# Expert weights laid out and requested in three pieces of 2 MB with runs of 16384 B, in place of six of 1 MB with runs of 8192 B

## What is computed

```python
def _moe(h, router_g, router_e, w1, w3, w2):
    ...
    expert = g_idx * E_PER_GROUP + e_idx          # each token: 2 of 32 experts
    ...
    def block(args):
        tok, e = args
        xb = h[tok]
        return (jax.nn.silu(xb @ w1[e]) * (xb @ w3[e])) @ w2[e]
    ...
    y = jnp.zeros((T, D_MODEL), jnp.float32).at[slot_tok].add(
        out.reshape(-1, D_MODEL).astype(jnp.float32) * slot_w[:, None])
```

## Time and profile before

| | us |
|---|---|
| median of 3 executions | 1469.42 (1469.12 to 1469.8) |
| the profiled execution, its time | 1473.97 |
| its span | 1472.1 |
| expert stage, from the first `up` to the last matmul of a block | 894.69 to 1422.53 |
| PE busy | 1368.9 (93%) |

### The profile page before, as it was taken

How to read it: one execution, slowest core, us unless ns; L and a number is a source line. 1 busy time by engine, 2 the same in 40 slices (tenths; PEclk the granted TensorE clock), 3 DMA queues, 4 the chain that set the end, 5 groups by cost and what they waited for, 6 DMA issues and landing times. The chain is left out here.

```text
span 1472.1 us, 33644 instructions
## 1 busy us (share of the span) xinstructions
PE 1368.9 (93%) x13661; PEld 960.7 (65%) x13661; DVE 671.2 (46%) x1362; ACT 309.4 (21%) x843; POOL 566.1 (38%) x452
## 2 busy tenths in 40 slices
PE   8999999998998999999999858999999989999864
PEld 4678888865566668887777534666666766666641
DVE  4757787842325567666667471112112111111127
ACT  1311011113113444443443100011001001100015
POOL 4212423402223235543334012445545544445435
PEclk9999999999998999999999979999999999999987
DMA  6334333244136232213321199999999999999936
GB/s 250 89 97 99 76 78 102 61 121 160 47 110 245 90 100 80 86 66 115 115 94 44 72 396 376 388 399 399 396 396 404 395 395 398 395 395 395 392 87 237
DMA packets 129606, 318.04 MB, mean 216 GB/s; under 512 B 48120, under 2 KB 86512, under 8 KB 103672
## 3 DMA queue, kind: packets, MB, share of 16 engines
q1 hardware_dynamic: 109720, 294.35, 53.3%
q0 software_dynamic: 18656, 18.15, 5.7%
q10 hardware_dynamic: 1152, 4.52, 0.8%
HBM read 277.05 MB, written 47.74 MB: 221 GB/s over the span
## 5 line engine op out<-in xcount | busy, mean ns | idle before, releaser
L2660 PE MATMUL bank<-sb_arena 128*32 128x256 f32 x6144 | 341.5, 381 | 12.2 <-DVE sb_arena L2768 5.7
L2660 PEld LDWEIGHTS bank<-sb_arena 128*32 128x32 f32 x6144 | 222.9, 111 | 125.4 <-issue 13.2
L515 PE MATMUL bank<-sb_arena 128*128 128x276 f32 x1008 | 235.0, 395 | 0.0
L2631 POOL DMA_INDIRECT d_acc<-sb_arena,sb_oidx x96 | 152.1, 1584 | 194.0 <-ACT sb_arena L2726 166.0
L515 PEld LDWEIGHTS bank<-sb_arena 128*128 128x128 f32 x1008 | 191.0, 190 | 44.0
L2676 PE MATMUL bank<-sb_arena 128*32 128x256 f32 x3072 | 172.9, 379 | 7.7 <-ACT sb_arena L2726 7.6
L2676 PEld LDWEIGHTS bank<-sb_arena 128*32 128x32 f32 x3072 | 110.6, 110 | 66.4 <-ACT sb_arena L2726 9.9
L2624 POOL DMA_INDIRECT sb_arena<-d_x,sb_idx x99 | 102.6, 1037 | 109.4 <-DVE sb_idx L2754 51.8
L2773 DVE TENSOR_SCALAR sb_oidx<-sb_slot 128x3 int32 x32 | 5.6, 174 | 286.1 <-DMA d_acc<-sb_arena,sb_oidx 285.7
L2726 ACT ACTIVATE sb_arena<-bank,sb_arena 128x256 f32<-128x256 f32 x96 | 38.5, 472 | 397.1 <-DVE sb_arena L2774 387.7
L1281 PE MATMUL bank<-sb_arena 128*128 128x512 f32 (+1 forms) x256 | 119.7, 596 | 0.0
(11 more groups left out here) (420 smaller groups left out, 1842.5 us busy)
## 6 DMA issues: line engine op xcount, KB each, us to landing
sb_arena<-w SPq DMA_DIRECT2D x192, 1024.0 KB, 28.1
sb_arena<-w_conv SPq DMA_DIRECT2D x28, 512.0 KB, 4.8
sb_arena<-d_conv SPq DMA_DIRECT2D x7, 1792.0 KB, 7.3
d_conv<-sb_arena SPq DMA_DIRECT2D x22, 512.0 KB, 3.3
sb_arena<-d_gam SPq DMA_DIRECT2D x8, 768.0 KB, 5.2
d_x<-sb_arena SPq DMA_DIRECT2D x9, 512.0 KB, 2.6
sb_arena<-xT ACTq DMA_DIRECT2D x8, 552.0 KB, 9.3
sb_arena<-w_out SPq DMA_DIRECT2D x8, 512.0 KB, 7.9
```

The lines of the kernel that those rows point to most:

```text
L515: last = e.matmul(bank[at + t][:, 0:HT // 2], weights[:, k, :], x[:, k, HT // 2 * t:HT // 2 * t + HT // 2], start=(k == 0), stop=(k == HK ...
L2631: e.indirect_dma_start(rows_out, bass.IndirectOffsetOnAxis(ap=oidx[:, r:r + 1], axis=0), eo[:, r, :], None, bounds_check=LAST_ROW, oob_is_ ...
L2660: mm = e.matmul(bank[UPB + r][j * CG:(j + 1) * CG, 0:2 * P], xgT[:, 2 * q + k, r * CG:(r + 1) * CG], w13[s][q][:, k, j, :], start=(q == 0 ...
```

## The change

The weights are laid out anew in memory, so that a request of 2 MB has one contiguous run of 16384 B for each partition. `w13` of an expert comes in two halves where it had four quarters, `w2` in one piece where it had two halves. SP waits until PE has passed the whole of the larger piece before it requests its refill, and PE waits once for each piece. The bytes, the order of the experts, the matmuls and the three sets stay. All else in the program is as it was.

```diff
-                    for q in range(4):
-                        e.dma_start(w13[s][q].rearrange("p k j n -> p (k j n)"), a["w13"][s, q]).then_inc(W["w13" + "abcd"[q] + str(s)], 16)
                     for h in range(2):
-                        e.dma_start(w2[s][h].rearrange("p k n -> p (k n)"), a["w2"][s, h]).then_inc(W["w2" + "ab"[h] + str(s)], 16)
+                        e.dma_start(w13[s][h].rearrange("p k j n -> p (k j n)"), a["w13"][s, h]).then_inc(W["w13" + "ab"[h] + str(s)], 16)
+                    e.dma_start(w2[s].rearrange("p k n -> p (k n)"), a["w2"][s]).then_inc(W["w2" + str(s)], 16)
...
                 def first_down(n, ex):
-                    for h in range(2):
-                        e.wait_ge(S["e_out"], 2 * (n - NSET) + h + 1)
-                        later2(h, n % NSET, ex)
+                    e.wait_ge(S["e_out"], 2 * (n - NSET) + 2)
+                    later2(n % NSET, ex)
...
                 for n in range(NSET, E1):
                     ex = expert(n)
-                    for q in range(4):
-                        e.wait_ge(S["e_up"], 4 * (n - NSET) + q + 1)
-                        later13(q, n % NSET, ex)
+                    for h in range(2):
+                        e.wait_ge(S["e_up"], 4 * (n - NSET) + 2 * h + 2)
+                        later13(h, n % NSET, ex)
...
                     for q in range(4):
-                        e.wait_ge(W["w13" + "abcd"[q] + str(s)], 16 * load)
+                        if q % 2 == 0:
+                            e.wait_ge(W["w13" + "ab"[q // 2] + str(s)], 16 * load)
...
+                    e.wait_ge(W[f"w2{s}"], 16 * load)
                     for h in range(2):
-                        e.wait_ge(W["w2" + "ab"[h] + str(s)], 16 * load)
...
-        "w13": np.stack([f["w1"][0], f["w3"][0]], 2).reshape(E, 4, 4, 2, CG, 2, 4, P).transpose(0, 2, 1, 4, 3, 6, 5, 7).reshape(E, 4, P, KT * 2 * P),
-        "w2": f["w2"][0].reshape(E, 4, 2, 2, CG, D).transpose(0, 2, 1, 4, 3, 5).reshape(E, 2, P, -1),
+        "w13": np.stack([f["w1"][0], f["w3"][0]], 2).reshape(E, 4, 2, 4, CG, 2, 4, P).transpose(0, 2, 1, 4, 3, 6, 5, 7).reshape(E, 2, P, 2 * KT * 2 * P),
+        "w2": f["w2"][0].reshape(E, 4, 4, CG, D).transpose(0, 1, 3, 2, 4).reshape(E, P, -1),
```

More of the change, by code:

```diff
@@ L159, in program @@
         S = sem_names
-        W = {n: nc.alloc_semaphore(name=n) for n in [f"w13{q}{s}" for q in "abcd" for s in range(NSET)] + [f"w2{h}{s}" for h in "ab" for s in range(NSET)]}
+        W = {n: nc.alloc_semaphore(name=n) for n in [f"w13{h}{s}" for h in "ab" for s in range(NSET)] + [f"w2{s}" for s in range(NSET)]}
         def sb(name, shape, dt=F32):
@@ L2266, in program @@
         A = Arena()
-        w13 = [[A(P, 2, 4, 2 * P) for _ in range(4)] for _ in range(NSET)]
-        w2 = [[A(P, 2, D) for _ in range(2)] for _ in range(NSET)]
+        w13 = [[A(P, 4, 4, 2 * P) for _ in range(2)] for _ in range(NSET)]
+        w2 = [A(P, 4, D) for _ in range(NSET)]
         ohp = A(P, 2 * NTT, BLK)
@@ L2316, in t4 @@
             return t.rearrange("p t (g e) -> p t g e", g=EG)
-        for n in ("w13a", "w13b", "w13c", "w13d"):
+        for n in ("w13a", "w13b"):
             nc.sync.sem_inc(W[f"{n}{UP_SET}"], 16 * AHEAD)
-        for n in ("w2a", "w2b"):
+        for n in ("w2",):
             nc.sync.sem_inc(W[f"{n}{DOWN_SET}"], 16 * AHEAD)
@@ L2599, in _ @@
                     ex = of(source, b, 0, E - 1)
-                    for q in range(4):
-                        e.wait_ge(S["e_up"], up_free + q)
-                        later13(q, UP_SET, ex)
+                    for h in range(2):
+                        e.wait_ge(S["e_up"], up_free + (2 * h + 1))
+                        later13(h, UP_SET, ex)
                     down_free = of(free2, e.snap(b - E1), 1, 2 * NBMAX)
                     before = of(source, e.snap(b - 1), 0, E - 1)
-                    for h in range(2):
-                        e.wait_ge(S["e_out"], down_free + h)
-                        later2(h, DOWN_SET, before)
+                    e.wait_ge(S["e_out"], down_free + 1)
+                    later2(DOWN_SET, before)
                 ex_end = of(source, e.snap(last - 1), 0, E - 1)
-                for h in range(2):
-                    e.wait_ge(S["e_out"], 2 * (E1 - NSET) + h + 1)
-                    later2(h, UP_SET, ex_end)
+                e.wait_ge(S["e_out"], 2 * (E1 - NSET) + 2)
+                later2(UP_SET, ex_end)
             @block.gpsimd
@@ L2696, in _ @@
                         for j in range(4):
[L2697 removed]
+                            mm = e.matmul(bank[UPB + NR - 1][j * CG:(j + 1) * CG, 0:2 * P], xgT[:, 2 * q + k, PAD:BLK], w13[UP_SET][q // 2][:, 2 * (q % 2) + k, j, :],
                                           start=(q == 0 and k == 0), stop=(q == 3 and k == 1))
@@ L2703, in _ @@
                     for j in range(4):
-                        mm = e.matmul(bank[LAST][j * CG:(j + 1) * CG, 0:256], hT[:, c, PAD:BLK], w2[UP_SET][c // 2][:, c % 2, j * 256:(j + 1) * 256],
+                        mm = e.matmul(bank[LAST][j * CG:(j + 1) * CG, 0:256], hT[:, c, PAD:BLK], w2[UP_SET][:, c, j * 256:(j + 1) * 256],
                                       start=(c == 0), stop=(c == 3))
```

25 lines of the change are left out of this document (10 added, 15 removed).

## The result

| | before | after |
|---|---|---|
| median | 1469.61 us (1469.12 to 1471.86, 4 runs) | 1523.17 us (1521.87 to 1524.06, 4 runs) |
| profiled execution, its span | 1472.1 us | 1522.2 us |

The ratio is 1.0368, with a 95% interval of 1.035 to 1.0385. The direction and the mechanism are those of the forecast. The size is not: 53.6 us, where 90 were forecast.

What follows compares the result with a forecast made beforehand. The ring of scatters was taken as the bound, PE 0.6 us below it. The profiled 1473.97 + 94.0 (27 turns at 19.6 instead of 16.12 us) - 3.4 = 1564.6, stated as 1560 us for the median, range 1467 to 1615.

Steps and rivals of the forecast that it cites:

- The bound, the ring, one packet for one: Expert stage: mark, evict, scatter and landing set 16.08 us a turn; each scatter packet waits for one weights packet.
- The faster rival: Expert stage: the scatter's wait does not grow with the run, turns stay at 16.1 us; 1464 us, chance 0.12.
- the one with split runs: Weights' queue: a 16384 B run is served as two 8192 B packets, so no change; about 1470 us, chance 0.10.
- the one in which the engines' total work sets 16.4 us a turn: Expert stage: the ring adapts and total DMA work is the bound; +5 us, 1474 us, chance 0.04.
- what I said the profile would show: Expert stage: 24 packets near 0.62 us, equal counts, issue to mark 17 to 18 us, PE waiting 4 us, about 325 GB/s.
- The turn beside a full stream: Expert stage, weights streaming all the time (f = 1): a turn of 23.1 us.
- The formula: Expert stage turn: T = 8.8 + 14.3 f, 8.8 us without the stream, f the share of time it runs.
- f = 14.9 / T, "the even spread": Expert stage: 14.9 us of weights work per turn, spread evenly over it, giving T = 19.6 us and +94.0 us over 27 turns.
- scatters that begin while the weights' queue is empty: Expert stage: burst phase to look for if the marks are right but the time is not.
- Its next matmuls are slower, but they lie within the wait: PE's clock may fall during its 4.1 us wait each turn; the slower matmuls were given no cost.
- The 3.4 us at the end: `up` of block 31: its 3.40 us mid-way wait for weights disappears with slower turns, -3.4 us.
- The coarser pieces, taken at nothing: Weights' requests: 2 MB pieces requested and usable later, costed at nothing, or 2.5 us once if cover were gone.

Runs made afterwards that it cites:

- the cut pair: Only the first of each block's three scatters kept, in both kernels: changed kernel 1446.46 us, kernel before 1444.27 us.
- runs of 4096 B: Kernel before, each 1 MB piece laid out and requested in runs of 4096 B instead of 8192 B: 1483.43 us, ratio 1.0087.
- 2 MB, old runs: Changed kernel's three 2 MB requests and waits, but the old layout with runs of 8192 B: 1478.42 us, ratio 1.0056.
- `w2` long: Kernel before, but `w2` in one piece with runs of 16384 B: 1491.49 us, ratio 1.014.
- changed, 12 requests: Changed kernel, each 2 MB piece asked for in four requests, each for every fourth partition: 1499.41 us, ratio 1.0221.
- `w13` long: `w13` in two pieces with runs of 16384 B, `w2` in halves as in the kernel before: 1508.62 us, ratio 1.0273.
- `w13` 32768 B: Changed kernel with `w13` in one 4 MB piece, runs of 32768 B: 1545.97 us, ratio 1.0514.
- 2 MB, old runs, halves: Changed kernel's 2 MB pieces with old 8192 B runs, each piece requested in two halves of neighbouring partitions: 1880.82 us, ratio 1.2803.
- changed, quarters: Changed kernel, each 2 MB piece asked for in four requests, each a quarter of neighbouring partitions: 1912.33 us, ratio 1.3029.
- the one with six late requests: Kernel before, its six 1 MB requests issued in pairs, as late as the changed kernel's three: 1469.85 us, ratio 1.0006.
- the cut kernel before: Kernel before with only the first of each block's three scatters: 1444.27 us, ratio 0.9834.

## Why the prediction was right in kind and too large in size

**The bound, the ring, one packet for one: right.** The waits are the same two, the counts stay equal with 16384-B packets where the stream is full (436 and 433, 82 and 81), and the cut pair shows that practically all of the loss goes through the scatter. The Trainium skill (DMA: Bandwidth & Descriptors, section "Queues, rings and completion order") would have an engine drain some 9 to 17 descriptors before it switches; by the profile's packets this is not what these queues do. The trace was the better guide. The faster rival (time below 1469) and the one with split runs are refuted by the result and by the packets' size; so is the one in which the engines' total work sets 16.4 us a turn. Of what I said the profile would show, the counts, the packet's length and the landing (9.7 us) came; GB/s fell to 366 and not to 325, from the issue to the next mark it is 6.6 to 22.4 us, 15.2 in the mean, and not 17 to 18, and PE waits for evict ten times, 0.5 to 7.7 us each, rather than 4 us in every turn.

**The turn beside a full stream: right.** The formula gave 8.8 + 14.3 = 23.1 us with f = 1, 21.3 of them from the issue to the mark; the scatter of 1128.29 took 21.16. With the mean packet in place of the data packet it gives the long turns of the other kernels too, with two exceptions. T = 8.8 + 7.2 x m / 0.284, with m the mean packet from the rows above, against the intervals of the marks in 1000 to 1380 us. The row of before is where the 7.2 us come from, and shows nothing by itself:

| kernel | m, us | T by formula | intervals, median |
|---|---|---|---|
| runs of 4096 B | 0.156 | 12.8, under PE's 15.54 | 15.5, until weights run short |
| before | 0.284 | 16.0 | 16.2 |
| 2 MB, old runs | 0.300 | 16.4 | 16.8 |
| `w2` long | 0.336 | 17.3 | 17.2 |
| changed, 12 requests | 0.421 | 19.5 | 19.7 (those over 18) |
| `w13` long | 0.429 | 19.7 | 19.4 (those over 18) |
| changed | 0.562 | 23.0 | 22.4 (those over 18) |
| `w13` 32768 B | 0.838 | 30.0 | 32 (one in four) |
| 2 MB, old runs, halves | 0.521 | 22.0 | 28.8, PE waits for weights |
| changed, quarters | 0.776 | 28.5 | 32.1 |

"Those over 18" are picked by their length and not by what ran beside them, so these rows show the size of the long turns, and not which turns are long. The formula is too low in the last two rows. In the first of them the weights are the limit: an expert's 6.29 MB take 30 us at 62.16 MB in 300. In the last one PE waits for evicts (107.9 us of 1000 to 1300) and not for weights, so there something more than the mean packet of the weights is slower in the ring, and it stays open what.

**The failed step: f = 14.9 / T, "the even spread".** It gave 19.6 us a turn; 18.26 were measured. Solved backwards, 18.26 = 8.8 + 14.3 f is f = 0.66 at most. The three scatters shown have (21.16 - 7.0) / 14.3 = 0.99, (17.95 - 7.0) / 14.3 = 0.77 and 0: a mean of 0.59. They aren't a lucky pick: over the 27 intervals that begin with the mark of 944.12 the mean is 15.2 us from the issue to the next mark, an f of 0.58, and seven of them lie within 6.6 and 7.7 us. The stream isn't spread evenly over a turn, it follows PE. A long turn makes PE wait; while PE waits nothing comes free and q1 runs dry some 4 us behind the wait's end (110 packets, of which ten behind 1101.5 us); and the evict that ends the wait lets a scatter go, most of whose packets meet the dry queue. Such a scatter lands in 6.64 us, the mark comes before the next evict asks for it, and the delay is paid back in part. The prediction had named this case ("scatters that begin while the weights' queue is empty") and its price with f = 0.6, 17.4 us a turn, but took the mean. 27 x (19.6 - 18.26) = 36.2 of the 40.6 us by which the forecast's own time (1564.6) lies over the 1524.01 of the profiled execution.

**Smaller terms.** "Its next matmuls are slower, but they lie within the wait" was wrong in place. The windows of PE's wait and of the first and second part of the `down` behind it (same columns as above) have a granted clock of 0.76, 0.50 and 0.96:

```profile
1092.00:1097.70 5.70, 0.00 (x1) 0.00 (x0) 0.82 (x3) 1.41 (x4) 0.07 (x1) 0.76 1.02 431
1097.70:1101.50 3.80, 3.76 (x36) 2.03 (x40) 0.11 (x1) 0.17 (x1) 3.19 (x3) 0.50 0.97 396
1101.50:1105.10 3.60, 3.60 (x68) 2.25 (x64) 2.50 (x6) 0.00 (x0) 2.63 (x3) 0.96 0.42 60
```

PE stood in the first; its first 36 matmuls ran at 1.2 GHz and the rest nearly all at 2.4. So that `down` took 7.34 us in place of 5.37, and this came behind the wait and not within it. The `up` behind it started later, POOL's third gather (1107.24, which waits for that `up`) was later, and the scatter queued behind it was issued 4.27 us after its mark in place of 1.80. This is why f comes out at 0.59 from the scatters and at 0.66 from the turn: over the same 27 intervals it is 2.64 us from the mark to the issue, so 0.8 us a turn are this delay, not the stream. This term was put at nothing and makes the turn longer, so it hid a part of the error in f.

**The 3.4 us at the end: about the right number, for the wrong reason.** The pause within the `up` of block 31 fell by 2.4 us, and the whole stretch behind the last turn by 4.3. But it isn't a wait for weights: its row names none (`<-issue`), and 154 of the 192 matmuls stand behind it, while the waits for weights stand ahead of the 1st, 49th, 97th and 145th. Nor do slower turns shorten it. The two cut kernels, both at 15.54 us a turn, have 3.0 us (before) and 0.6 us (changed), the kernel with `w2` long, whose `w13` comes in four quarters as before, has 0.4, and the one with six late requests 2.9. The term was right by luck, and what the pause is stays open. The remaining 3.4 us between the spans lie ahead of block 2's `down`, which began that much earlier. They need no cause in the change: the cut kernel before has before's program up to the first scatter, and its `down` of block 0, ahead of that scatter, starts at 909.99 us, where before's starts at 918.33 and the changed kernel's at 912.40.

**Two readings of the kernel before.** The window of the earlier trace rows begins with the `up` of block 2 at 923.51, not with its `down`; the idle time in it is the same. And the 16.12 us of the earlier trace rows are a mean of unlike turns of PE. Its first nine, to 1089.43, take 15.56 us each while the marks are already 15.5 to 16.8 us apart: PE still has a lead on the ring. One turn, 1202.07 to 1222.52, takes 20.45, as POOL issues a gather 8.92 us behind the one before it, and the `up` waits 3.00 us for the gate and takes 12.25 in place of 10.55; what holds POOL there isn't in the rows. That the mean lies so near to the ring's 16.08 is in part luck. The ring as the bound stands on the marks, which are 16.3 us apart in the mean of 1000 to 1380 us.

**The coarser pieces, taken at nothing, cost 8.9 us.** Later requests cost nothing, as foreseen (1.0006). PE did not wait for weights in the 2 MB kernel, as foreseen. What I had missed stood in my own count, "each landing request also brings 16 tiny packets": in q1 too these are turns, and cheap ones. Six requests an expert have 6 in 54 of them, three have 3 in 51. By the formula this is 0.4 us a turn, 11 us; measured were 8.9 us in the median, which is 0.33 us a turn (0.53 between the profiled executions, of which that of the 2 MB kernel was a slow one). As transfers they are next to nothing: the tiny packets of the earlier trace rows take about 0.01 us each, and not the 0.06 us of an expectation above. With 16384-B runs the counts show it (230 to 234, 78 of them tiny), and the time moved that way (12 requests for 3: -23.8 us, with the changed order of partitions in it). For the 8.9 us it is argued from there and from what the other runs leave; the kernel that would have shown it directly, 2 MB pieces with old runs in requests for every second partition, was not run.

## What to carry to other kernels

Where a plain stream and an indirect scatter share the DMA engines, as here, the scatter pays one packet of the stream for each of its own. The stream's run length sets the scatter's latency, and longer runs are bought with it unless the scatter is off the path. Look at what waits for the small queue before lengthening the big one's runs. Here the scatter's ring was the bound by 0.6 us a turn with 8192 B and by 2.7 with 16384 B, and with 4096 B the stream was. And a stream that follows the engine it delays is not spread evenly: work out the stalled turn and the turn behind it apart.

## What the runs showed of the hardware

- Two busy queues get packet for packet alike, at 16384 B (436 to 433) and at a few bytes (116 to 117), and the closing packets of a request count as turns (230 to 234, 78 of them tiny). Behind a stretch in which the weights' queue had been empty, q0 got more (408 to 314).
- Requests for 64 or for 32 neighbouring partitions move 62.16 and 63.15 MB in 300 us, with q1's share at 93%, where 108.75 had moved. Requests for every fourth partition, also 32 of them, move 109.18. The Trainium skill (SBUF — State Buffer, section "Door 1: The DMA port swizzle (why `[64,N]` ≈ `[32,N]`)") has 0 to 31 and 0 to 63 on the same 8 of 16 ports. By that map both splits should cost the same and every fourth partition should reach all ports, and the bytes moved agree with each; the ports themselves are in no trace. Its further advice, in the section "Can I just issue two DMAs to hit both halves?", that only one transfer over all 128 partitions reaches all 16, is not what the last run shows.
- With the number and size of the data packets unchanged, four times the requests, each for every fourth partition, made the changed kernel 24 us faster (1523.17 to 1499.41). More requests are not only overhead.
